# A pool opening, a norm schedule and one weight sum put in another order in a fused decoder layer

## What is computed

```python
h = rmsnorm(x, g_pre_mix)
p = h @ w_in            # columns xv | B | C | u | gate_conv | gate_pool
A = (B * causal_dwconv3(C * xv)) @ w_out_conv
Bp = pool_scale * groupwise_linear(trailing_mean_w(u) - u)   # w = 2, 4, 8, 16
mix = (sigmoid(gate_conv) * A + sigmoid(gate_pool) * Bp) @ w_o
x = x + rmsnorm(mix, g_post_mix)
f = square(relu(rmsnorm(x, g_pre_mlp) @ w_up)) @ w_down
x = x + rmsnorm(f, g_post_mlp)
```

## Time and profile before

| | |
|---|---|
| runs of the kernel before | 943.41, 949.11, 1122.82 us |
| median | 949.11 us |
| the profiled execution | 948.61 us |
| its span (core 4, the slowest) | 947.6 us |
| spans of the other cores | 937.0 to 944.2 us |
| busy on core 4 | PE 97%, DVE 68%, ACT 39%, POOL 13% |
| DMA | 122.35 MB, 129 GB/s in the mean |

### The profile page before, as it was taken

One profiled execution on the slowest core, in us unless ns is written; L12 is line 12 of the kernel. 1 busy time (PEld: TensorE's weight loads), 2 busy tenths in 40 slices (PEclk: granted clock), 3 DMA queues, 4 the chain that ended last, 5 costly groups with the idle time before them and its releaser, 6 DMA issues.

```text
span 947.6 us, 15567 instructions; the slowest of 8 cores (937.0 to 947.6 us)
## 1 busy us (share of the span) xinstructions
PE 918.6 (97%) x5079; PEld 449.8 (47%) x5079; DVE 642.5 (68%) x967; ACT 373.2 (39%) x755; POOL 122.5 (13%) x170
## 2 busy tenths in 40 slices
PE   7899999999999999999999999699999999999997
PEld 5654444444545455454544344244444545544443
DVE  3767766774677776678778888467677665556187
ACT  3343432222444445333335777330224665520213
POOL 5120000000122120000000011100040121120022
PEclk9999999999999999999999999899999999999999
DMA  9999967735475946303695789994394457095026
GB/s 194 236 254 163 162 87 124 185 67 90 89 139 119 171 87 111 56 11 59 151 264 188 122 128 169 61 175 94 96 236 148 78 91 134 1 154 113 1 94 262
DMA packets 60222, 122.35 MB, mean 129 GB/s; under 512 B 31472, under 2 KB 31728, under 8 KB 59888
## 3 DMA queue, kind: packets, MB, share of 16 engines
q0 software_dynamic: 19872, 73.41, 45.3%
q1 hardware_dynamic: 39984, 47.66, 19.9%
q10 hardware_dynamic: 288, 0.30, 0.1%
HBM read 161.05 MB, written 19.01 MB: 190 GB/s over the span
## 4 chain that ended last, share of the span: by engine, by line
PE 86%; DMA 6%; DVE 3%; issue 2%; ACT 1%; POOL 0%; SPq 0%; DVEq 0%; ACTq 0%; POOLq 0%
PE PS L139 86%; DMA AR<-AR 5%; DVE AR L159 2%; DMA AR<-x_p 2%; DVE AR L169 1%; ACT AR L156 1%; POOL AR L129 0%; DVE AR L164 0%; SPq L534 0%; DVEq L224 0%; ACT STAT L156 0%; DVE STAT L428 0%; PE PS L143 0%; DVE AR L175 0%; ACTq L224 0%
## 5 line engine op out<-in xcount | busy, mean ns | idle before, releaser
L139 PE MATMUL PS<-AR 128*128 128x512 bf16 (+1 forms) x4992 | 908.0, 345 | 19.5 <-ACT AR L156 7.1
L139 PEld LDWEIGHTS PS<-AR 128*128 128x128 bf16 x4992 | 443.6, 98 | 482.8 <-issue 27.9
L159 DVE TENSOR_TENSOR AR<-AR 128x1024 bf16<-128x1024 bf16 (+11 forms) x277 | 233.4, 862 | 74.8 <-PE PS L139 28.8
L156 ACT ACTIVATE AR<-PS 128x512 f32<-128x512 f32 (+3 forms) x266 | 156.6, 601 | 297.8 <-PE PS L139 259.8
L159 DVE TENSOR_TENSOR AR<-PS,AR 128x512 f32<-128x512 f32 (+2 forms) x249 | 158.7, 649 | 141.8 <-PE PS L139 126.8
L156 ACT ACTIVATE AR<-AR 128x512 bf16<-128x512 f32 (+3 forms) x163 | 113.3, 715 | 81.8 <-DVE AR L159 52.3
L169 DVE SCALAR_TENSOR_TENSOR AR<-AR,CS 128x512 f32<-128x512 f32 (+1 forms) x80 | 66.2, 827 | 36.2 <-ACT AR L156 17.3
L159 POOL TENSOR_TENSOR AR<-AR 128x1024 f32<-128x1024 f32 (+1 forms) x25 | 48.2, 1928 | 301.0 <-DVE AR L169 92.2
L156 ACT ACTIVATE AR<-PS,CS 128x512 f32<-128x512 f32 (+1 forms) x80 | 49.0, 621 | 76.8 <-PE PS L139 67.4
L156 ACT ACTIVATE AR<-AR,CS 128x512 f32<-128x512 f32 (+1 forms) x40 | 26.3, 657 | 102.1 <-DVE AR L159 102.1
L169 DVE SCALAR_TENSOR_TENSOR AR<-AR,STAT 128x1024 bf16<-128x1024 f32 (+2 forms) x51 | 60.6, 1201 | 6.4 <-DVE STAT L428 1.6
(11 more groups left out here) (38 smaller groups left out, 81.7 us busy)
## 6 DMA issues: line engine op xcount, KB each, us to landing
AR<-w_dn POOLq DMA_DIRECT2D x32, 512.0 KB, 18.4
AR<-w_m POOLq DMA_DIRECT2D x16, 768.0 KB, 9.4
AR<-w_up POOLq DMA_DIRECT2D x16, 768.0 KB, 8.6
AR<-x_p SPq DMA_DIRECT2D x18, 512.0 KB, 9.9
x_d<-AR SPq DMA_DIRECT2D x17, 512.0 KB, 4.3
AR<-x_d SPq DMA_DIRECT2D x17, 512.0 KB, 7.6
AR<-x_p POOLq DMA_DIRECT2D x14, 512.0 KB, 18.5
AR<-w_a POOLq DMA_DIRECT2D x24, 256.0 KB, 20.3
```

Source lines behind the costliest of these rows:

```text
L139: return self.add("pe", lambda e: e.matmul(out, lhsT, rhs, start=start, stop=stop, **kw), reads=[lhsT, rhs], writes=[out], signal=sig, nam ...
L156: return self.add("act", lambda e: e.activation(out, in_, func, **kw), reads=rd, writes=wr, name=name)
L159: return self.add(eng, lambda e: e.tensor_tensor(out, in0, in1, op), reads=[in0, in1], writes=[out], name=name)
```

## The change

It has four parts.

1. HN gets an eighth buffer, at byte 169152, for the second half, and the nine tiles are put over the buffers in another way. The norms inside the first half's up steps are given half steps: the list `slots` has one entry for each `mid`, the square of a tile is emitted one half step ahead of its product and transpose.
2. `up_sums(0, 1)`, the weight sums of the second block of the first half, is emitted in step 1 behind part 1, instead of at the end of step 0.
3. `phase_b` opens by token group and then by channel, instead of by channel and then by group.
4. The opening is one step where it was two. Tile 4's norm is put ahead of everything that follows the first group; the norms of tiles 5, 6 and 7 are split into the square (`x_sq`) and a scaling on ACT (`x_scale`) in place of the product on DVE; the pieces of the three chains are written out by hand in another order. GM's load waits for the load of tile 7 instead of tile 4. The step numbers that loads refer to go down by one, which leaves the loads where they were.

```diff
-        HN_.append([arv(b_, BF16, [D]) for b_ in (89280, 91328, 72896, 74944, 135168, 137216, 98304)])
+        HN_.append([arv(b_, BF16, [D]) for b_ in (89280, 91328, 72896, 74944, 135168, 137216, 98304, 169152)])
...
+        def x_sq(i):
+
+            ss = x_ss[i] = stat()
+            P.act(XN[i % 3], XS[i], AF.Square, accum_out=ss, name="sq")
+            rstd_from(ss)
+
+        x_ss = {}
+
+        def x_scale(i):
+            P.act(XN[i % 3], XS[i], AF.Identity, scale=x_ss[i], name="xn")
+
...
-            a_pair((0, 0, bk[0]), (1, 0, bk[1]), (4, lambda: x_norm(4)), (8, lambda: x_norm(5)))
-            for t in bk:
-                for b in t:
-                    drop(b)
-        step(a_keys(0, 0) + a_keys(0, 1), head)
-
-        def head3():
-            bk = (bank(), bank(), bank())
-            a_mm(2, 0, bk, None, (0, 1))
+            x_norm(4)
+            p, q = a_chain(0, 0, bk[0]), a_chain(1, 0, bk[1])
+            p[0]()
+            p[1]()
+            x_sq(5)
+            q[0]()
+            q[1]()
+            drop(bk[0][0])
+            drop(bk[0][1])
             x_tr(4)
-            a_mm(2, 0, bk, None, (2,))
-            x_norm(6)
+            p[2]()
+            x_scale(5)
+            q[2]()
+            p[3]()
+            p[4]()
+            p[5]()
+            x_sq(6)
+            b2 = (bank(), bank(), bank())
+            a_mm(2, 0, b2, None, (0, 1))
             x_tr(5)
-            a_ew(2, 0, bk)
-            x_norm(7)
-        step(a_keys(0, 2), head3)
+            a_mm(2, 0, b2, None, (2,))
+            c = a_chain(2, 0, b2)
+            c[0]()
+            q[3]()
+            q[4]()
+            q[5]()
+            x_scale(6)
+            c[1]()
+            c[2]()
+            x_sq(7)
+            drop(bk[0][2])
+            for b in bk[1]:
+                drop(b)
+            for fn in c[3:]:
+                fn()
+            x_scale(7)
+        step(a_keys(0, 0) + a_keys(0, 1) + a_keys(0, 2), head)
...
-            for j in range(2):
-                for tg in tgs:
+            for tg in tgs:
+                for j in range(2):
                     step([("u", h, 0)], lambda j=j, tg=tg: u_unit(j, tg))
...
-                    HN_[v][i % 5 if i < 8 else (0, 3, 4, 2, 0, 4, 1, 5, 6)[i - 8]])
+                    HN_[v][i % 5 if i < 8 else (0, 2, 4, 3, 5, 7, 1, 0, 6)[i - 8]])
...
+            if (half, p) == (0, 1):
+                up_sums(half, 1)
             if mid:
                 mid.pop(0)()
...
-                if n < 7:
+                if n < 7 and (half, n) != (0, 0):
                     up_sums(half, n + 1)
...
+        slots = (None, 11, 9, None, 13, 15, None, 12, 16, 10, None)
+
+        def norm_slot(q):
+
+            if slots[q] is not None:
+                s_b2b(slots[q])
+            if slots[q + 1] is not None:
+                s_b2a(slots[q + 1])
+
...
-                        ts_ = ((11, 9), (13,), (15,), (16, 12), (10,))[p - 1]
-                        up_step(half, p, mid=[lambda ts_=ts_: [s_b2a(t) for t in ts_], lambda ts_=ts_: [s_b2b(t) for t in ts_]])
+                        up_step(half, p, mid=[lambda q=q: norm_slot(q) for q in (2 * p - 2, 2 * p - 1)])
...
-        P.dma("sp", GM, bcast(g_pre_mix), "gm", deps=[xload[4]])
+        P.dma("sp", GM, bcast(g_pre_mix), "gm", deps=[xload[7]])
```

More of the change, by code:

```diff
@@ L545, in build_program @@
                     for c in range(3):
-                        loads[("a", h, j, c)] = dict(n=1, early=max(0, min(j - 1, 3)) if j > 2 else 0)
+                        loads[("a", h, j, c)] = dict(n=1, early=max(0, min(j - 1, 2)) if j > 2 else 0)
                 else:
@@ L707, in build_program @@
             for g in range(4):
-                loads[("u", h, g)] = dict(n=2, early=3)
+                loads[("u", h, g)] = dict(n=2, early=2)
             for m in range(8):
-                loads[("m", h, m)] = dict(n=3, early=3)
+                loads[("m", h, m)] = dict(n=3, early=2)
                 if h == 1 and m >= 6:
@@ L1442, in build_program @@
         first((0, 0), (0, 1), (0, 2), 2, (1, 0), (1, 1), 3, (1, 2), (2, 0), 4, (2, 1), 5, (2, 2), 6, 7)
-        P.dma("sp", GM, bcast(g_pre_mix), "gm", deps=[xload[4]])
+        P.dma("sp", GM, bcast(g_pre_mix), "gm", deps=[xload[7]])
         first((3, 0), (3, 1), (3, 2), 8, 9, 10, (4, 0), (4, 1), (4, 2))
-        S_X = 3
+        S_X = 2
         for s, st in enumerate(steps):
```

## The result

The changed kernel needs 935.78 us (median, 933.34 the fastest) beside 948.21 us for the kernel before on the same chip: a ratio of 0.9875, 95% interval 0.9831 to 0.9919. Forecast were 935.6 us and a range of 931.5 to 947.0. By the 2% bound that is no change; by the interval it is faster.

A forecast was written before the change was run, and what follows sets the result against it. TensorE, busy 918.6 of 947.6 us, on the slowest core was taken as the bound. Core 2's 938.0 less 3.4 (0.5 opening, 1.3 pool, 1.6 up steps) is 934.6, plus 1.0 gives 935.6 us; range 931.5 to 947.

The forecast's parts named there:

- The removed wait: Near 600 us, ACT no longer waits for tile 12's transpose; 7.1 + 2.3 us on core 4, nothing on core 2.
- Core 4 undisturbed: Core 4 without late transpose, lower clock and later wait: 947.6 - 7.1 - 2.3 - 1.3 = 936.9 us.
- Tile 16: Its transpose, second in line, lands at 611.4 or 608 us, before DVE's relu-square in step 8 wants its buffer.
- Sums and norm slots: First half's up steps: moved sums together with new norm slots gain 1.6 us, bounds 0 and 2.85.
- two stalls of 0.53: Up steps: steps 3 and 5 hold two norms each, so two PE stalls of 0.53 us were left.
- Pool opening: First pooling units near 122 us: PE's stall falls from 1.43 to 0.1; gain 1.3 us, bounds 0.9 and 1.43.
- Opening: Up to PE's slice of tile 6: DVE's eviction 6 ends at 45.1 against 45.73; gain 0.5 us, bounds -1 and +2.
- eviction 4 at 31.2: Opening: adding durations one after the other, DVE's eviction of tile 4 ends at 31.2 us.
- the slowest core becomes core 2: 938.0 - 3.4: Whole span: with no late transpose core 2 is slowest, and each core's gain of 3.4 gives 934.6 us.
- rival (a): Down phase: the stall returns as DVE's last sums wait for late w_down pieces; 940 to 948 us, chance 0.30.
- (b): Step 8: tile 16's transpose lands near 623.3 and holds back DVE; 949.2 us, range 942 to 965, chance 0.05.
- (c): Near 600 us: another transpose under act_at blocks, so the wait is not removed; 944 us, chance 0.03.
- (d): Opening loses 1 us, sums and pool opening give half; 938.6 us, chance 0.10; sign: tile 6's slice later than 45.9.

The follow-up runs named there:

- oldbufs: Changed kernel with tile 12 back in the buffer at 89280 and tile 15 at 137216; one execution, cores 930.7 to 933.4 us.
- before_gate: Kernel before, with the last two pieces of w_down's third quarter waiting for tile 10's transposes; 938.85 us, ratio 0.9925.
- after_again: The changed kernel, unaltered, measured once more on another chip; 934.86 us, ratio 0.9868.
- part1: Kernel before with only the new norm buffers and norm slots; 941.76 us, ratio 0.9934.
- part2: Kernel before with only the second block's weight sums moved one step on; one execution, cores 936.7 to 942.6 us.
- part3: Kernel before with only the pool opening by token group; one execution, 0.9 us gained at the pool opening, no total time given.
- dn_gate: Changed kernel, with the last two pieces of w_down's third quarter waiting for tile 10's transposes; 934.17 us, ratio 0.9873.
- gm4: Changed kernel with the gain load behind tile 4 of x instead of tile 7; one execution, cores 930.6 to 934.3 us.
- evac_first: Changed kernel with the third chain's last three pieces emitted behind tile 6's eviction, banks held; 943.01 us, ratio 0.9924.

## Why the prediction was right, and where it was not

**The removed wait.** Right, as a mechanism and in size. Core 4 undisturbed was put at 7.1 + 2.3 + 1.3 = 10.7 us less; its D is 11.2 above the undisturbed value. The slowest core went from one with a late transpose to one without. What I did not see is that the order alone would do it (oldbufs), and so would the gate (before_gate).

**Tile 16.** It was forecast at 608 to 611 and called tight; it lands at 593.0 to 597.7 in the first profile, and at 606.1 on the struck core 2 of after_again, where DVE did not wait for it either. The step took the second landing of before for the second of after. But tile 12 goes out alone where two tiles did, and the second now lands about where the first did (596 to 599). That the half step between them is the reason was not tried apart.

**Sums and norm slots: the mis-sized term.** Forecast 1.6 (bounds 0 to 2.85), measured 3.2. Two things failed. I counted two norms in steps 3 and 5 and left two stalls of 0.53 behind them; part1 shows none. Before, both norms of a step stood right ahead of the sums; on core 2 of before (DVE):

```profile
564.24 0.69 DVE L159 TENSOR_TENSOR AR<-PS,AR 128x512 f32<-128x512 f32 x1 [1.47 <-PE PS L139]
...
567.18 1.28 DVE L169 SCALAR_TENSOR_TENSOR AR<-AR,STAT 128x1024 bf16<-128x1024 f32 x1
568.38 0.16 DVE L874 RECIPROCAL STAT<-STAT 128x1 f32<-128x1 f32 x1
568.66 1.29 DVE L169 SCALAR_TENSOR_TENSOR AR<-AR,STAT 128x1024 bf16<-128x1024 f32 x1
569.86 2.88 DVE L159 TENSOR_TENSOR AR<-AR 128x1024 bf16<-128x1024 bf16 x4
```

After, one is in each half, and the one in the first half falls where DVE had idled for PE (1.47 us before 564.24). It was not the number of norms in a step that made the stall, but their standing together ahead of the sums. The second is smaller: the idles add to 2.85, the gain is 3.2, so a stop costs PE more than its idle row shows, here 0.1 us each. The same comes out of part1 (idle 1.74, C 1.8 over after) and of part2 (idle 1.50 + 0.53, C 2.3 over).

**Pool opening.** Forecast 1.3, measured 1.6 (B), and 1.3 against before_gate. The edit named for it gives 0.9 alone, not 1.3. The working had the second operation done at 120.6, just ahead of PE's need, and took that for the end of the wait. But in its own rows PE starts 0.34 us after this operation (121.07 + 0.69 to 122.10), and part3 shows the operation itself 0.2 us later than assumed, behind an idle of 0.52. Some 0.5 more comes from part 4, which the working had priced only at tile 6's slice. The size came out near by luck.

**Opening.** Forecast 0.5, measured 0.4 to 1.1 in A, whose spread over cores is larger than the gain. PE's slice of tile 6 was forecast to start near 45.2; it starts at 45.35 in the mean of the eight cores (44.19 to 46.46). That was called a gain of 0.5 because core 4 started it at 45.87 before. But core 4 was the earliest: the eight cores of before have 45.87 to 47.59, mean 46.67, so this start moved by 1.3 (by 0.8 between before_gate and dn_gate). Part of it is lost again to the clock, which the working put at nothing. It was right that the stretch at 1.2 GHz near 38 is hidden: from the slice of tile 6 to matmul 800 every core of before with all its records takes 71.19 us. But the new stops of 1.27 and 0.52 stand right ahead of that slice, and behind them nothing hides a lower clock. On core 7, where it fell (0.58 and 0.56 over 46 to 50), the same stretch takes 72.81 us, 1.6 more. Fourteen of the 64 core traces of the eight kernels with this opening have it (1 in after, 2 in after_again, 3 in gm4). Why only some was not found.

The step "eviction 4 at 31.2" came at 31.9 on core 7. DVE took it up at 30.65, behind the second chain's z, whose copy on ACT stood behind the square of tile 5, and that had waited 1.11 us for its tile (27.91). PE's product for the third chain waits for this eviction, which the sum did not hold. Eviction 6 ended at 46.05 there, not 45.1. ACT's scaling pass takes 1.14 us, not the 1.05 of the sum, a small part of this. The Trainium skill (ScalarE: Activation LUTs, What ACT_TABLE_LOAD costs) gives an ACTIVATE 186 ns and 0.833 ns per column, and 280 ns as the fixed part with one pointer operand; the estimate from it is 1.04 and 1.13 us for 1024 columns. The rows agree, 1.04 to 1.06 for the square and 1.14 to 1.15 for the scaling pass.

**From one core to eight.** Per core the change gives 4.9 (dn_gate against before_gate) to 5.9 us (after against before) instead of 3.4, yet the time is the one forecast. The failed step is "the slowest core becomes core 2: 938.0 - 3.4". It takes the slowest core to be like the undisturbed ones of before (937.0 to 938.0). After, the eight cores have a mean of 931.4 and the slowest is 2.3 above it, through A alone (118.99 on core 7, 115.38 to 117.29 on the five others with all records): its slice of tile 6 starts 0.8 later than the mean, and the lower clock behind it costs 1.6. In other executions rival (a) does it now and then. Two errors of about 2 us nearly cancelled.

**The rivals.** (a) was right as a mechanism: of 24 core traces of after, after_again and gm4, two show it, with 3.91 and 1.03 us. Its chance was for the slowest of eight cores, so executions count. One core stood 3 us or more over the median of its eight in one of nine executions of the changed kernel, but in six of nine of evac_first (up to 946.1 us) and six of ten of part1 (up to 952.9), whose edits leave w_down alone, and in none of the ten with the gate. That leaves 0.30 and 948 neither too heavy nor confirmed. (b) and (c) appear in no trace: no DVE or ACT wait for a transpose between 560 and 670 us on any core of the changed kernel. The sign named for (d), the slice of tile 6 later than 45.9, stands on cores 4, 6 and 7 (46.11, 46.46, 46.18), although the opening gained in the mean; it was set by core 4, the earliest of before.

## What to carry over

When small transfers that someone waits for share the DMAs with bulk loads that have slack, look at who can be held back: one dependency of a weight piece on the last transpose moved its landing from 599 to 612 (after_again) down to 588 to 593, and in the kernel before from 603 to 627 down to 594 to 597. Split short vector work over the places where its engine idles rather than by count per step, and judge a move together with the one that makes room for it (0.97 and 1.43 apart, 3.25 together). For a time that the slowest of eight cores sets, forecast a core's gain and the spread among the cores separately, and read the state before from all eight. Where a stop moves, ask again whether a lower clock behind it would be hidden.

## What the runs showed of the hardware

A DMA transpose of one tile lands 3.0 us after issue alone. Beside weight pieces it takes 12 to 43 us on the cores of before, after and after_again, 29.6 to 42.8 on core 4 of before, and holding back two pieces of 512 KB made the last one land in 5.6 on core 2. Over 590 to 605 on core 2 of after_again, with transposes and weights both under way, the DMAs' share is 1.15, but they moved 78 GB/s, against 131 over the whole span of after (windows; the columns are those of the earlier trace rows):

```profile
590.00:605.00 15.00, 15.00 (x72) 6.75 (x70) 7.93 (x12) 9.47 (x18) 2.12 (x4) 1.00 1.15 78
```

The gate also shows that the weights lose little by waiting: their last piece lands at 619.7 to 624.3 with it, and at 619.8 to 631.7 without.

A stop of PE costs about 0.1 us beyond its idle row (C of before, part1 and part2 against after). A stretch at 1.2 GHz right behind a stop costs nothing where another engine ends last (71.19 us from tile 6's slice to matmul 800 on every such core of before) and 1.6 us where PE does (72.81 on core 7 of after).
